# The two heads of a pair share TensorE's array: values, neighbourhood scores and linear-attention products in a two-part transformer kernel on one Trainium2 core

## What is computed

```python
def log_decay(z_lr, w_alpha, b_alpha):
    z = jnp.einsum('bldr,drk->bldk', z_lr.reshape(B, L, 2, GLA_GATE_RANK), w_alpha) + b_alpha
    ...
def gla_chunked(q, k, v, log_a, s0):
    ...
    att = jnp.where(incl, jnp.einsum('bnihd,bnjhd->bnhij', q_dec, k_inv), 0.0)
    o_intra = jnp.einsum('bnhij,bnjhv->bnihv', att, vc)
    ...
    o_inter = jnp.einsum('bnihd,nbhdv->bnihv', q_dec, s_prev)
    return (o_intra + o_inter).reshape(B, L, H, dv)
def neighborhood_attention(q, k, v, k_ctx, v_ctx, rpb):
    ...
    s_loc = jnp.einsum('brqhd,brkhd->bhrqk', qg, kb).astype(jnp.float32) * scale + bias
    ...
    s_ctx = jnp.einsum('brqhd,bkhd->bhrqk', qg, k_ctx).astype(jnp.float32) * scale
    p = jax.nn.softmax(jnp.concatenate([s_loc, s_ctx], axis=-1), axis=-1).astype(v.dtype)
    o = (jnp.einsum('bhrqk,brkhd->brqhd', p[..., :n_loc], vb)
         + jnp.einsum('bhrqk,bkhd->brqhd', p[..., n_loc:], v_ctx))
def mla_branch(...):
    p = jax.nn.softmax(s.astype(jnp.float32) * scale, axis=-1).astype(v.dtype)
    return jnp.einsum('bhqk,bkhd->bqhd', p, v)
```

## Time and profile before

| | |
|---|---|
| median of 3 runs | 3114.51 us (3114.46 to 3116.63) |
| the profiled execution | 3117.43 us, its span 3115.6 us |
| PE busy | 2952.5 us (95%), 13132 matmuls |
| weight loads busy | 2298.8 us (74%) |
| DVE, ACT, POOL busy | 1419.1, 1203.0, 1217.3 us |
| mean granted TensorE clock | 0.971 |
| DMA | 278.08 MB, mean 89 GB/s |

### The profile page before, as it was taken

The page is one execution under the profiler, slowest core; times in us unless marked ns, Lnnn a source line. Parts: engine busy times, 40 slices in busy tenths (PEclk is TensorE's granted clock), DMA queues, the critical chain, the costliest instruction groups (busy, mean ns, idle before and its releaser), DMA issues.

```text
span 3115.6 us, 33638 instructions
## 1 busy us (share of the span) xinstructions
PE 2952.5 (95%) x13132; PEld 2298.8 (74%) x13132; DVE 1419.1 (46%) x1887; ACT 1203.0 (39%) x1737; POOL 1217.3 (39%) x555
## 2 busy tenths in 40 slices
PE   8998999999999898999998999989899999999997
PEld 4787777778888666677786888866666777778886
DVE  5657542441112778664525202267877353151123
ACT  4237643342223554342334323253533433342232
POOL 1112223344445344353443544434434434344442
PEclk9999999999999999999999999989999999999998
DMA  6333221332223210122131322222011222322221
GB/s 229 109 115 116 75 71 65 114 110 95 101 95 108 95 55 28 48 88 88 68 128 59 111 95 95 101 95 74 29 48 61 88 81 83 114 82 96 100 95 61
DMA packets 89342, 278.08 MB, mean 89 GB/s; under 512 B 10048, under 2 KB 10176, under 8 KB 89184
## 3 DMA queue, kind: packets, MB, share of 16 engines
q1 hardware_dynamic: 89184, 275.92, 25.1%
HBM read 268.54 MB, written 7.34 MB: 89 GB/s over the span
## 4 chain that ended last, share of the span: by engine, by line
PE 78%; DVE 15%; ACT 4%; issue 2%; DMA 1%; POOL 1%; SPq 0%; DVEq 0%; ACTq 0%; POOLq 0%
PE bank L1400 23%; PE bank L1402 22%; PE bank L1401 22%; PE bank L1609 2%; DVE pageF L2295 2%; PE bank L1451 1%; PE bank L1584 1%; PE bank L1572 1%; PE bank L1561 1%; DVE pageF L2103 1%; DVE pageF L2373 1%; DVE pageF L2369 1%; DMA pageF<-in_wmod 1%; DVE pageR L2168 1%; PE bank L1600 1%
## 5 line engine op out<-in xcount | busy, mean ns | idle before, releaser
L2405 POOL TENSOR_TENSOR wlo<-wraw,whi 128x1024 fp32r<-128x1024 f32 x429 | 1046.9, 2442 | 1630.2 <-ACT whi L1636 1625.4
L1400 PE MATMUL bank<-pageR,whi 128*128 128x512 f32 x3552 | 1449.7, 408 | 70.4 <-ACT pageR L1793 27.4
L1402 PE MATMUL bank<-pageR,wlo 128*128 128x512 f32 x3552 | 1385.0, 390 | 0.0
L1401 PE MATMUL bank<-pageR,whi 128*128 128x512 f32 x3552 | 1384.6, 390 | 0.0
L1400 PEld LDWEIGHTS bank<-pageR,whi 128*128 128x128 f32 x3552 | 676.4, 190 | 258.8 <-issue 112.2
L1401 PEld LDWEIGHTS bank<-pageR,whi 128*128 128x128 f32 x3552 | 677.3, 191 | 150.2 <-issue 23.8
L1402 PEld LDWEIGHTS bank<-pageR,wlo 128*128 128x128 f32 x3552 | 675.6, 190 | 141.2
L1636 ACT ACTIVATE whi<-wraw 128x1024 fp32r<-128x1024 f32 x429 | 450.6, 1053 | 412.1 <-PE bank L1402 407.4
L1676 ACT ACTIVATE pageR<-pageF 128x512 fp32r<-128x512 f32 x136 | 85.9, 632 | 425.0 <-DVE pageF L2162 208.1
L2295 DVE SCALAR_TENSOR_TENSOR pageF<-pageF,prm 128x497 f32<-128x497 f32 (+9 forms) x180 | 205.2, 1140 | 1.8
L1755 ACT ACTIVATE pageF<-bank,smal 128x512 f32<-128x512 f32 x96 | 66.0, 687 | 205.0 <-DVE smal L2077 204.7
(11 more groups left out here) (199 smaller groups left out, 2350.6 us busy)
## 6 DMA issues: line engine op xcount, KB each, us to landing
wraw<-in_wst SPq DMA_DIRECT2D x429, 512.0 KB, 3.4
pageF<-in_wmod SPq DMA_DIRECT2D x96, 256.0 KB, 4.8
pageF<-in_xT SPq DMA_DIRECT2D x16, 256.0 KB, 5.0
pageF<-in_bias SPq DMA_DIRECT2D x16, 256.0 KB, 3.8
kept<-pageF SPq DMA_DIRECT2D x16, 256.0 KB, 4.7
pageF<-kept SPq DMA_DIRECT2D x16, 256.0 KB, 4.2
pageF<-tables SPq DMA_DIRECT2D x8, 256.0 KB, 4.7
out_x<-pageF SPq DMA_DIRECT2D x8, 256.0 KB, 2.0
```

The source lines that it names most:

```text
L1400: e.matmul(o, hi, xh, start=first, stop=False)
L1401: e.matmul(o, hi, xl, start=False, stop=False)
L1402: i = e.matmul(o, lo, xh, start=False, stop=last)
L2405: e.tensor_tensor(wlo[:, b % NH, :, :], wraw[:, b % NR, :, :], bc(whi[:, b % NH, :, :]), ALU.subtract).then_inc(*wlod.up(("wlo", b)))
```

## The change

The two heads of a pair are planned and issued together. `na_scores(m, qt)` takes both heads' banks and issues the four products in turn between the row halves. `na_values(m, qt)` and `mla_values(l, j, qt)` issue eight products in turn between the column halves, and only when the probabilities of both heads are there. The order of jobs becomes pair, query block, head. `gla_scores(m, dr)` and `gla_out(m)` issue both heads' products (the 64-row ones in turn between the row halves), `gla_gate` is split in one call for the tokens and one for the context, with the two directions on rows 0 to 31 and 32 to 63 (the low-rank weights are laid out twice for that). The scores of the latent attention are issued as before, one job at a time. No product is added or left out. The core of the diff:

```diff
     def side_gla():
...
-            for hp in range(2):
-                h = 2 * m + hp
-                for dr in range(2):
+            pair = (2 * m, 2 * m + 1)
+            for dr in range(2):
+                for h in pair:
                     sbk.take(("ab", h, dr))
                     pages.take(("am", h, dr))
-                    step("gla_scores", m, hp, dr)
+                step("gla_scores", m, dr)
+                for h in pair:
                     sbk.give(("ab", h, dr), ("am", h, dr))
                 yield
+            for h in pair:
                 sbk.take(("ob", h))
                 pages.take(("og_raw", h))
-                step("gla_out", m, hp)
+            step("gla_out", m)
...
     def side_na():
+        def scores(job):
             h, qt = job
+            if h % 2:
+                return
...
+            for x in (h, h + 1):
+                sbk.take(("sc", "na", (x, qt)))
+            step("na_scores", h // 2, qt)
...
         def after(job):
             h, qt = job
             m = h // 2
-            if h % 2 == 0 and qt == 0:
+            if h % 2 == 0:
+                return
+            if qt == 0:
                 sbk.take(("nab", m))
-            step("na_values", h, qt)
+            step("na_values", m, qt)
...
-        jobs = [(h, qt) for h in range(8) for qt in range(4)]
+        jobs = [(2 * m + hp, qt) for m in range(4) for qt in range(4) for hp in range(2)]
...
-            jobs = [(l, h, qt) for h in range(8) for qt in range(4)]
+            jobs = [(l, 2 * j + hp, qt) for j in range(4) for qt in range(4) for hp in range(2)]
...
-            def gla_gate(m, dr):
-                g = (m, dr)
-                wt = wal[:, dr, 128 * m:128 * m + 128]
...
+            def gla_gate(m):
...
+                for dr in range(2):
+                    rows = slice(32 * dr, 32 * dr + 32)
+                    clear(("zb", (m, dr)))
+                    e.matmul(bank(("zb", (m, dr))), wal[rows, 128 * m:128 * m + 128], F(("z",))[rows, :],
+                             start=True, stop=True).then_inc(*dot.up(("zb", (m, dr))))
...
+            def gla_scores(m, dr):
...
                 for j in range(4):
                     sl = slice(128 * j, 128 * j + 128)
-                    i = e.matmul(o[:, sl], k[rows, sl], q[rows, sl], start=True, stop=True)
-                i.then_inc(*dot.up(("ab", h, dr)))
+                    for hp in range(2):
+                        rows = slice(64 * hp, 64 * hp + 64)
+                        i = e.matmul(bank(("ab", 2 * m + hp, dr))[:, sl], k[rows, sl], F(("E1", g))[rows, sl],
+                                     start=True, stop=True)
+                i.then_inc(*dot.up(("ab", 2 * m, dr), ("ab", 2 * m + 1, dr)))
...
+            def gla_out(m):
...
                     for c in range(8):
                         sl = slice(64 * c, 64 * c + 64)
-                        i = e.matmul(o[:, sl], state(g, c)[rows, :], F(("E1", g))[rows, sl], start=False,
-                                     stop=dr == 1 and c == 7, skip_group_check=True)
+                        for hp, h in enumerate(pair):
+                            rows = slice(64 * hp, 64 * hp + 64)
+                            i = e.matmul(bank(("ob", h))[:, sl], state(g, c)[rows, :], F(("E1", g))[rows, sl],
+                                         start=False, stop=dr == 1 and c == 7, skip_group_check=True)
...
+            def na_scores(m, qt):
...
+                for part in range(2):
+                    for hp, sc in enumerate(scs):
+                        rows = slice(64 * hp, 64 * hp + 64)
+                        k = F(("knc", m))[rows, 0:256] if part else F(("kn", m))[rows, k0:k0 + 256]
+                        i = e.matmul(bank(sc)[:, 256 * part:256 * part + 256],
+                                     F(("qn", m))[rows, 128 * qt:128 * qt + 128], k, start=True, stop=True)
+                i.then_inc(*dot.up(*scs))
...
-            def mla_values(l, h, qt):
...
+            def mla_values(l, j, qt):
+                o, V = bank(("mlab", l, j)), F(("mv", l, j))
+                if qt == 0:
                     clear(("mlab", l, j))
                 w.wait_ge(*when("mv", l, j))
-                w.wait_ge(*when("pt", "mla", (l, h, qt)))
+                for hp in range(2):
+                    w.wait_ge(*when("pt", "mla", (l, 2 * j + hp, qt)))
                 for c in range(4):
-                    i = e.matmul(o[f, 128 * qt:128 * qt + 128], V[:, 128 * c + 64 * hp:128 * c + 64 * hp + 64],
-                                 P[:, 128 * c:128 * c + 128], start=c == 0, stop=c == 3)
-                i.then_inc(*dot.up(("av", "mla", (l, h, qt)), ("mlab", l, j)))
+                    for hp in range(2):
+                        i = e.matmul(o[64 * hp:64 * hp + 64, 128 * qt:128 * qt + 128],
+                                     V[:, 128 * c + 64 * hp:128 * c + 64 * hp + 64],
+                                     F(("pt", "mla", (l, 2 * j + hp, qt)))[:, 128 * c:128 * c + 128], start=c == 0,
+                                     stop=c == 3)
+                i.then_inc(*dot.up(("av", "mla", l, j, qt), ("mlab", l, j)))
```

More of the change, by code:

```diff
@@ L611, in na_values, with attention @@
         made.add(("vn", m))
-    def attention(kind, jobs, ready, before, after, middle=lambda job: None):
+    def attention(kind, jobs, ready, scores, after, middle=lambda job: None):
         n = len(jobs)
@@ L619, in attention @@
                     yield
-                before(jobs[i])
-                sbk.take(("sc", kind, jobs[i]))
-                step(kind + "_scores", *jobs[i])
+                scores(jobs[i])
             if 1 <= i <= n:
@@ L664, in after @@
             m = h // 2
-            if h % 2 == 0 and qt == 0:
+            if h % 2 == 0:
+                return
+            if qt == 0:
                 sbk.take(("nab", m))
-            step("na_values", h, qt)
-            pages.give(("pt", "na", job), ("av", "na", job))
-            if h % 2 == 1 and qt == 3:
+            step("na_values", m, qt)
+            for x in (h - 1, h):
+                pages.give(("pt", "na", (x, qt)), ("av", "na", m, qt))
+            if qt == 3:
                 pages.take(("o_na_f", m))
@@ L958, in after @@
                 j = h // 2
-                if h % 2 == 0 and qt == 0:
+                if h % 2 == 0:
+                    return
+                if qt == 0:
                     sbk.take(("mlab", l, j))
-                step("mla_values", l, h, qt)
-                pages.give(("pt", "mla", job), ("av", "mla", job))
-                if h % 2 == 1 and qt == 3:
+                step("mla_values", l, j, qt)
+                for x in (h - 1, h):
+                    pages.give(("pt", "mla", (l, x, qt)), ("av", "mla", l, j, qt))
+                if qt == 3:
                     pages.take(("o_mla_f", l, j))
@@ L984, in maker, with scores @@
                 pages.give(("kpe", l), ("kpd", l, 7))
+            def scores(job):
+                sbk.take(("sc", "mla", job))
+                step("mla_scores", *job)
             mk = maker()
-            jobs = [(l, h, qt) for h in range(8) for qt in range(4)]
-            for _ in attention("mla", jobs, lambda job: job[1] // 2 in live, lambda job: None, after):
+            jobs = [(l, 2 * j + hp, qt) for j in range(4) for qt in range(4) for hp in range(2)]
+            for _ in attention("mla", jobs, lambda job: job[1] // 2 in live, scores, after):
                 next(mk, None)
@@ L1501, in gla_states @@
                 i.then_inc(*dot.up(("u", g)))
[L1503 to L1507 removed]
+            def gla_scores(m, dr):
+                g, k = (m, dr), F(("la", (m, dr)) if dr else ("P", (m, dr)))
+                for hp in range(2):
+                    clear(("ab", 2 * m + hp, dr))
                 w.wait_ge(*when("qd", g))
@@ L1554, in na_values @@
+                i.then_inc(*dot.up(*scs))
+            def na_values(m, qt):
+                o = bank(("nab", m))
+                if qt == 0:
                     clear(("nab", m))
```

211 lines of the change are left out of this document (101 added, 110 removed).

## The result

| | before | changed |
|---|---|---|
| median of the runs | 3114.49 us (3113.9 to 3116.63) | 3071.26 us (3068.63 to 3075.01) |
| ratio | | 0.9861, interval 0.9844 to 0.9878 |
| span of the profiled execution | 3115.6 us | 3069.0 us |
| PE busy | 2952.5 us | 2867.2 us |
| PE idle, sum of all gaps | 138 us | 176 us |

A forecast was written before the change was run, and what follows sets the result against it. PE, busy 95% of the span, was taken as the bound, with DVE setting the pace in two latent stretches. Savings of 19.7 + 20.0 + 19.7 + 4 + 3.6 + 7.9 + 2.1 = 77.0 us gave 3037.5 us, range 3018 to 3072.

The forecast's parts named there:

- items 1 to 6: Neighbourhood values, scores, latent values, linear-attention scores, outputs, gates: savings of 19.7, 20.0, 19.7 + 4, 3.6, 7.9, 2.1 us.
- Items 2, 4 and 5: Neighbourhood scores, linear-attention scores and 64-row outputs: row halves overlap, saving 20.0, 3.6 and 7.9 us.
- row halves don't overlap: Rival: row halves with full-width weights don't run side by side, the load path being shared; 3064.8 us, chance 0.12.
- column sides don't overlap: Rival: in neighbourhood and latent values, merged calls save only the switch; 3069.7 us, chance 0.03.
- item 4: Linear-attention scores: 16 of a pair's 32 pass slots go at 0.11 us, 1.8 us a pair, 3.6 in all.
- item 6: Gates: rows 0 to 31 beside 32 to 63 halve L1468's 4.3 us, saving 2.1 us.
- items 1, 2: Neighbourhood attention: a pair's values or scores cost what one head's did, saving 19.7 and 20.0 us.
- item 7: Held banks in neighbourhood attention, and the new job order: costed at nothing, since ACT is half idle.
- rows 8: Profile rows of busy time by stretch; from 330 to 520 us PE is busy 189.9 of 190 us.
- item 3: Latent values: 19.7 us saved outside the stretches that DVE fills, 2 us a layer inside, 4 in all.
- The PE time turns into waits: Rival: in the fed stretches other engines, held banks or values awaiting both heads stall PE, eating half; 3076 us, chance 0.13.
- the clock rival: Rival: the granted clock falls in the fed stretches; at 200 us of lower level 3131 us, chance 0.04.

The follow-up runs named there:

- E1: The changed kernel with one more empty turn (yield) of the side chain behind the linear-attention outputs; 3061.34 us.
- E7: E1 with the output bank of neighbourhood attention taken from the four banks of the linear products; 3056.49 us.
- E8: The changed kernel with two more empty turns (yields) of the side chain behind the linear-attention outputs; 3062.55 us.
- E4: The kernel before with only the latent attention's values in pairs, and the job order they need; 3099.66 us.
- E9: E7 with the latent output bank also taken from the four banks of the linear products; 3057.33 us.
- E12: E4 with DVE's convolution taps and POOL's fourth-tile sums cut to 8 columns, and the latent output bank moved as in E9; 3055.63 us.
- E3: The changed kernel with the same merged calls, but all products of the first head before those of the second; 3094.98 us.
- E10: The kernel before with DVE's convolution taps and POOL's sums of the fourth tile cut to 8 columns; 3078.71 us.
- E6: E4 with DVE's share of the convolution cut to 8 columns; 3083.04 us.

## Why the prediction was right, and where it was off

The direction and the overlaps were right, the size was not: 43 us for 77. The median lies 0.7 us inside a range that reached to 3072 in order to hold the two rivals of missing overlaps. Both are refuted, so that the range held is luck. The items below are those of the prediction.

1. **The overlaps (items 1 to 6).** Right, each of them. Items 2, 4 and 5 rested on rows of another shape, and held; the rivals "row halves don't overlap" (a scores pair would have cost 2 x 1.25 - 0.35 = 2.15 us, it cost 1.27) and "column sides don't overlap" fell with the first timeline. For the rule of the Trainium skill ("TensorE: Matmul & The Clock Gate", Part 3: Packing small matmuls), that a weight load overlaps matmuls under way only where its row group differs, the trace says no: the values' two sides share all rows and ran side by side, and the second side's first weight load (1109.531 to 1109.664 us) lies beside the first side's pass from 1109.526 on. That by this rule column sides "would gain nothing" was my inference and not the page's: the table of the same part has 2.38x for three column tiles.
2. **Linear attention and gates.** Forecast 13.6 us, 12.1 there by the lead at 241 us, 16.5 in E1. Two small slips stand in the terms: item 4 took 0.11 us from the row of the outputs, where its own row gives (2.05 - 0.27) / 15 = 0.12, and item 6 left out the context products (L1471); the gates saved 2.6 us in place of 2.1.
3. **Neighbourhood attention (items 1, 2).** Forecast 39.7; the lead rose by 17.8 from 241 to 532 us, in E1 by 28.1, in E7 by 32.2. The failing step is in item 7 and in the reading of rows 8: I took the stretch from 330 to 520 us, where PE has no gap, for all of neighbourhood attention. Its preparation from 240 to 320 us is a chain of norms, transposes and first jobs, in which PE already waited before. There a shorter PE step brings little by itself, and a shift in the order of the side chains costs (E1, E8). No term of the sum stood for that, though the prediction's own sign of being wrong, new waits of PE for evictions by ACT, came (8.26 us).
4. **"I cost this at nothing" (item 7).** Roughly right, for a reason that was wrong. The banks do make waits (22.7 us of them in E7's latent stretch), but they covered other waits; taking them away gave about 5 us at neighbourhood attention and nothing at latent attention.
5. **Latent values (item 3).** Forecast 19.7 + 4 = 23.7; E4 shows 16 by the medians and 17.6 by its leads, the changed kernel 18.5 by its leads. The failing term is the 4. Outside the two stretches that DVE fills (1130 to 1210 us and 2190 to 2270) E4's lead rises by 20.5 us, near the 19.7 forecast; inside them it falls by 2.9, where I had it rise by 2 a layer. DVE's load (32 of 50 us in the fed part, 74 of 80 after it) belongs to the same jobs, so what PE saved in front is partly waited off there. With DVE and POOL relieved the same edit gives 25. "What is late next there is DVE" was right; its price was too low.
6. **The rival that came.** "The PE time turns into waits", 3076, given 0.13, stood 5 us from the result. It was right that DVE and ACT would be late. Its place was wrong: the fed stretches lost next to nothing (from 360 to 480 us PE is busy 118.9 of 120), the thin ones did. The Trainium skill's "TensorEngine Tiling (Array Packing)", PSUM Bottleneck, points to the emptying of banks as what comes next; here it was, at the first gap, ACT's place in the queue rather than its share of time (39%).
7. **The clock** stayed at 1.00 in the fed part and cost nothing there. From 241 to 532 us as a whole it cost at most 8 us more than before, behind the gaps; the clock rival looked for it in the fed part alone.

In sum, of the 34 us that are missing, some 22 went between 241 and 532 us (10 of them back in E1, 4 more in E7), 5 to 6 in the latent stretches, and the rest in small steps elsewhere. The 22 are longer gaps of PE (16.9 us more) and the lower clock behind them. Which step of the preparation makes these gaps stays open: the norms on ACT, the late modulation weights and the chain of the first jobs were not taken apart. The best versions are E7 and E9, which don't differ (3056.5 and 3057.3 us, some 60 less than the kernel before beside them).

## What to carry to other kernels

- Time saved on the bounding engine counts only where that engine has no gaps. Go through the stretches around the saving as well: where it waited before, a shorter step only makes it wait longer, and a shift in order can cost more than the saving. Then try a neighbouring phase before judging a change; here one empty turn was worth 10 us beside a gain of 43. And look in its trace whether the wait that it was meant to end is gone: in E8 it was not, and the time was as good.
- A wait's releaser names the last of several covers. Before a bank or buffer is blamed, look at what would end the wait next (E9), and take both away at once (E12).
- For two halves of the array to work together, alternate their products in program order. Otherwise, in this kernel, the second half began only when three passes of the first were left to start (E3).

## What the runs showed of the hardware

- **How far ahead TensorE looks.** Chains of 8 passes on two column sides: 1.23 us alternated, 1.71 one after the other (E3). Chains of 4 passes: 1.27 us either way. In all four shapes of E3 the second half's first pass starts when three passes of the first half have not started yet: behind the fifth of eight (values, and linear-attention scores on row halves), behind the first of four (neighbourhood scores), behind the thirteenth of sixteen (linear-attention outputs). So a pass started beside those of the other half from four places behind in the queue, and not from further.
- **A DVE operation can stand still beside POOL.** Eight columns took 0.22 us by themselves and up to 2.41 us beside POOL's subtractions of 2.4 us (E10). Of these 180 operations, the 124 with no POOL operation beside them took at most 0.23 us; the 28 that took over 1 us all ended 0.02 or 0.03 us after one of POOL's. Two lines of E6, DVE, with the least, median and longest duration in ns: the maximum of the scores, which reads a bank, and the normalisation of the probabilities, which reads and writes SBUF:

```profile
L2082 DVE TENSOR_REDUCE smal<-bank x96: 675/691/694, 294.0 to 2268.3; 128x1 f32<-128x512 f32 x96
```

```profile
L2091 DVE TENSOR_SCALAR pageF<-pageF,smal x96: 485/487/2394, 299.1 to 2270.8; 128x512 f32<-128x512 f32 x96
```

The first hardly varies, the second goes from 0.49 to 2.39 us. The Trainium skill's "SBUF — State Buffer" (SBUF: two separate sides) says why: the two engines share a pair of ports, which one instruction holds until it is done, when DVE's operation has two inputs in SBUF or runs in a two-port mode. The trace agrees, as far as it shows the inputs; whether an operation ran in such a mode it doesn't show. So DVE's share of busy time isn't all work here, and fewer columns don't shorten the part that is spent standing still.
